# Keeping permuted token rows and gathering them as quarter rows for VectorE block transposes, in a pooling and expert-choice MoE layer

## What is computed

```
h = concat([meta, x])                        # 2064 x 1024
u = rmsnorm(h, norm_mix)
h = h + pool_mixer(u) * pool_scale           # windows 2, 4, 8, 16, then a 256x256 weight per group
u = rmsnorm(h, norm_ffn)
aff = softmax(u @ router_w)                  # 2064 x 16
for each expert e:
    g, idx = top_k(aff[:, e], 258)
    xs = u[idx]                              # 258 x 1024: the gathered rows
    hid = silu(xs @ w_gate[e]) * (xs @ w_up[e])      # 258 x 2048
    h[idx] += (hid @ w_down[e]) * g
return rmsnorm(h, norm_final)[16:]
```

## Time and profile before

| | |
|---|---|
| time, median of three runs | 2460.56 us |
| the profiled execution: its time | 2459.51 us |
| the profiled execution: its span | 2457.7 us |
| PE busy | 2386.0 us, 97% |
| PE weight loads busy | 2228.7 us, 91% |
| DVE busy | 1866.3 us, 76% |
| ACT busy | 1204.2 us, 49% |
| POOL busy | 850.4 us, 35% |
| DMA | 486.11 MB, mean 198 GB/s |

### The profile page before, as it was taken

The page is one execution under the profiler, slowest core; times in us unless marked ns, Lnnn a source line. Parts: engine busy times, 40 slices in busy tenths (PEclk is TensorE's granted clock), DMA queues, the critical chain, the costliest instruction groups (busy, mean ns, idle before and its releaser), DMA issues.

```text
span 2457.7 us, 48606 instructions
## 1 busy us (share of the span) xinstructions
PE 2386.0 (97%) x17338; PEld 2228.7 (91%) x17338; DVE 1866.3 (76%) x2259; ACT 1204.2 (49%) x1938; POOL 850.4 (35%) x1013
## 2 busy tenths in 40 slices
PE   7958999999999999999999999999999999999997
PEld 7947989898999989899998989899998989899997
DVE  5666786868787786968788686968778686968775
ACT  5653444444444444454444444454544444454464
POOL 0001525234251524335251524335152533425111
PEclk9968999999999999999999999999999999999998
DMA  7664648485765758586774848586674848576594
GB/s 239 213 194 128 185 135 257 151 244 183 212 198 154 227 148 251 159 237 173 204 214 140 246 139 248 160 239 188 181 216 136 253 142 251 171 227 199 159 346 164
DMA packets 345810, 486.11 MB, mean 198 GB/s; under 512 B 23117, under 2 KB 294997, under 8 KB 345778
## 3 DMA queue, kind: packets, MB, share of 16 engines
q1 hardware_dynamic: 318370, 433.82, 57.9%
q0 software_dynamic: 23232, 36.67, 6.9%
q10 hardware_dynamic: 4176, 15.21, 1.6%
HBM read 443.27 MB, written 46.31 MB: 199 GB/s over the span
## 4 chain that ended last, share of the span: by engine, by line
PE 87%; issue 3%; DVE 1%; POOL 1%; ACT 1%; DVEq 0%; POOLq 0%; ACTq 0%
PE bank L1498 86%; PE bank L1503 1%; ACT marks_a L910 0%; POOL fin L785 0%; POOL h_rows L793 0%; DVE w_lo L1340 0%; DVE h_rows L1459 0%; POOL fin L781 0%; POOL out L814 0%; DVE key_t L1223 0%; DVE x_lo L1345 0%; DVE y_rows L1450 0%; DVE marks_v L1197 0%; DVE flag L1204 0%; DVE cand L1210 0%
## 5 line engine op out<-in xcount | busy, mean ns | idle before, releaser
L1498 PE MATMUL bank<-x_hi,w_hi 128*128 128x258 f32 x4096 | 1156.8, 282 | 1.5 <-DVE x_lo L1345 1.5
L1498 PE MATMUL bank<-x_lo,w_hi 128*128 128x258 f32 x4096 | 1158.1, 283 | 0.0
L1498 PE MATMUL bank<-x_hi,w_lo 128*128 128x258 f32 x4096 | 1156.4, 282 | 0.0
L1340 DVE TENSOR_TENSOR w_lo<-raw,w_hi 128x1024 fp32r<-128x1024 f32 x584 | 713.9, 1223 | 116.5 <-ACT w_hi L932 91.0
L1498 PEld LDWEIGHTS bank<-x_hi,w_hi 128*128 128x128 f32 x4096 | 776.7, 190 | 15.0 <-issue 12.6
L1498 PEld LDWEIGHTS bank<-x_hi,w_lo 128*128 128x128 f32 x4096 | 778.1, 190 | 0.0
L1498 PEld LDWEIGHTS bank<-x_lo,w_hi 128*128 128x128 f32 x4096 | 777.4, 190 | 0.6
L932 ACT ACTIVATE w_hi<-raw 128x1024 fp32r<-128x1024 f32 x581 | 612.1, 1054 | 311.5 <-PE bank L1498 290.9
L668 POOL TENSOR_TENSOR carrier<-carrier 128x1 f32<-128x1 f32 x360 | 112.6, 313 | 1130.3 <-ACT y_rows L983 446.4
L713 POOL DMA_INDIRECT list_rows<-pair_now,slot_now x285 | 410.7, 1441 | 136.5 <-issue 135.6
L1366 DVE SCALAR_TENSOR_TENSOR acc_left<-raw,hid_left,acc_left 128x1024 f32<-128x1024 f32 x330 | 422.1, 1279 | 0.0
(11 more groups left out here) (209 smaller groups left out, 1893.1 us busy)
## 6 DMA issues: line engine op xcount, KB each, us to landing
raw<-in_moe_w_down SPq DMA_DIRECT2D x98, 1024.0 KB
raw<-in_moe_w_gate SPq DMA_DIRECT2D x97, 1024.0 KB
raw<-in_moe_w_up SPq DMA_DIRECT2D x97, 1024.0 KB
raw_more<-in_moe_w_gate SPq DMA_DIRECT2D x31, 1024.0 KB
raw_more<-in_moe_w_up SPq DMA_DIRECT2D x31, 1024.0 KB
raw_more<-in_moe_w_down SPq DMA_DIRECT2D x30, 1024.0 KB
h_in<-in_x SPq DMA_DIRECT2D x18, 512.0 KB, 5.7
h_acc<-h_mid SPq DMA_DIRECT2D x17, 448.0 KB, 4.9
```

The costliest lines, as they stand in the source:

```text
L1340: nc.vector.tensor_tensor(w_lo[:, a % 4], split_view(a, last), w_hi[:, a % 4].bitcast(f32), ALU.subtract).then_inc(split_lo, 1)
L1498: return nc.tensor.matmul(dst, lhs, rhs, start=start, stop=stop)
```

## The change

Rows of u are stored with their channels permuted. In the norm (DVE, stage one) four instructions of 256 columns write what one of 1024 wrote, and the router's weights are loaded in the same order by 16 DMAs. A row is seen as 4 quarters of 256 numbers. Nine indirect DMAs gather 128 quarter rows each (partition 32 i + c takes quarter i of token c of a group of 32) into `x_lanes`, which has the place of `x_rows`. DVE turns 32x32 blocks with three transposes of 128x768 (`turn_lanes`), after rows 10, 11 and 12 of `down`; ACT rounds (`round_lanes`, rows 11 to 13) and DVE subtracts (`rest_of_lanes`, rows 12 to 14) from SBUF. PE turns nothing of the gathered rows. The indices are quarter indices, `idx_lanes`: for the first expert 20 short instructions make them, later the list is read back with 10 DMAs instead of 3. `read_list` stands after row 1's `split_rest` and no longer ahead of row 0's work.

```diff
+GROUPS = 9
+PIECE = 3
...
-    u_chunks = u_rows.rearrange("t (m c) -> (t m) c", c=P)
+    u_quarters = u_rows.rearrange("t (i w) -> (t i) w", i=4)
...
-        x_rows = sb("x_rows", [P, 2, D], f32)
+        x_lanes = sb("x_rows", [P, GROUPS * 256], f32)
+        x_rows = x_lanes[:, 0:2 * D].rearrange("p (b d) -> p b d", b=2)
...
+        x_t = sb("x_t", [P, 2, PIECE * 256], f32, all_but_last)
...
+        def by_chunk(rows):
+            return rows.rearrange("p (i k r) -> p k i r", i=4, k=KD)
+        def in_order(rows):
+            return rows.rearrange("p (k i r) -> p k i r", i=4, k=KD)
...
-            sp.dma_start(rw[:], router_w[0].rearrange("(k p) e -> p k e", p=P)).then_inc(loaded_c, 16)
+            with nc.allow_non_contiguous_dma(reason="rows of 16 numbers"):
+                for j in range(4):
+                    for i in range(4):
+                        sp.dma_start(rw[32 * j:32 * j + 32, 2 * i:2 * i + 2, :],
+                                     router_w[0].rearrange("(h j i r) e -> j i r h e", h=2, j=4, i=4)[j, i])\
+                          .then_inc(loaded_c, 16)
...
-            def gather(first=False):
-                for b in range(2):
-                    pool.indirect_dma_start(x_rows[:, b, :], None, u_rows,
-                                            bass.IndirectOffsetOnAxis(ap=idx[:, b:b + 1], axis=0))\
-                        .then_inc(gathered[b], 16)
-                if first:
-                    pool.wait_ge(list_ready, 3)
-                pool.indirect_dma_start(x_left[0:SMALL_ROWS, :], None, u_chunks,
-                                        bass.IndirectOffsetOnAxis(ap=idx_chunk[0:SMALL_ROWS, :], axis=0))\
-                    .then_inc(gathered[2], 16)
+            def gather_lanes(first=False):
+                for g in range(GROUPS):
+                    if first and g % 8 == 0:
+                        pool.wait_ge(lanes_listed, 17 + g // 2)
+                    pool.indirect_dma_start(x_lanes[:, g * 256:(g + 1) * 256], None, u_quarters,
+                                            bass.IndirectOffsetOnAxis(ap=idx_lanes[:, g:g + 1], axis=0))\
+                        .then_inc(lanes_gathered[g // PIECE], 16)
...
-                    for t in range(LEFT):
-                        pool.dma_start(listed_rows[t:SMALL_ROWS:LEFT, 2, :],
-                                       list_rows[256 + t].partition_broadcast(KD)).then_inc(list_read, 16)
+                    pool.dma_start(listed_rows[0:LEFT, 2, :], list_rows[256:CAP, :]).then_inc(list_read, 16)
+                    for i in range(4):
+                        at = 32 * i
+                        pool.dma_start(listed_lanes[at:at + 32, 0:8, :],
+                                       list_rows[0:256, :].rearrange("(g c) v -> c g v", c=32)).then_inc(list_read, 16)
+                        pool.dma_start(listed_lanes[at:at + LEFT, 8, :], list_rows[256:CAP, :]).then_inc(list_read, 16)
...
-                pool.wait_ge(x_turned, XT * n + XT)
+                pool.wait_ge(lanes_turned, XP * n + XP)
                 carry_wait()
-                gather()
+                gather_lanes()
...
-            def round_x(i, done, at=0):
-                act.wait_ge(x_turned, done)
-                nc.scalar.activation(x_part(x_hi, i), turned_x(i, at), ACT.Copy).then_inc(x_hi_done, 1)
-            for i in range(XT):
-                round_x(i, i + 1, 4)
+            def round_lanes(m, p):
+                at = slice(96 * p, 96 * p + 96)
+                act.wait_ge(lanes_turned, XP * m + p + 1)
+                nc.scalar.activation(x_hi_wide[:, :, at].rearrange("p k (g c) -> p k g c", g=PIECE),
+                                     x_t[:, p % 2].rearrange("p (g k c) -> p k g c", g=PIECE, k=KD),
+                                     ACT.Copy).then_inc(x_hi_done, 1)
+            for p in range(XP):
+                round_lanes(0, p)
...
-                    if 8 <= k < 8 + XT:
-                        round_x(k - 8, XT * n + XT + k - 7)
+                    if 11 <= k < 11 + XP:
+                        round_lanes(n + 1, k - 11)
...
-                    nc.vector.scalar_tensor_tensor(out=u_out[:, s % 2, :], in0=h_mid[:, s % 2, :],
-                                                   scalar=inv2[:, s:s + 1], in1=nffn[:], op0=ALU.mult,
-                                                   op1=ALU.mult).then_inc(normed, 1)
+                    for i in range(4):
+                        ins = nc.vector.scalar_tensor_tensor(out=by_chunk(u_out[:, s % 2, :])[:, :, i],
+                                                             in0=in_order(h_mid[:, s % 2, :])[:, :, i],
+                                                             scalar=inv2[:, s:s + 1], in1=in_order(nffn[:])[:, :, i],
+                                                             op0=ALU.mult, op1=ALU.mult)
+                    ins.then_inc(normed, 1)
...
+                dve.wait_ge(list_ready, 1)
+                dve.wait_ge(lanes_listed, 1)
+                for i in range(4):
+                    for g in range(4):
+                        nc.vector.tensor_scalar(idx_lanes[32 * i:32 * i + 32, g:g + 5:4], idx[32 * g:32 * g + 32, 0:2],
+                                                4.0, float(i), ALU.mult, ALU.add).then_inc(lanes_listed, 1)
...
+                nc.vector.scalar_tensor_tensor(out=idx_lanes[:], in0=listed_lanes[:, :, 0], scalar=4.0,
+                                               in1=lane.broadcast_to([P, GROUPS]), op0=ALU.mult,
+                                               op1=ALU.add).then_inc(list_ready, 1)
...
-            def rest_of_x(i, count_, at=0):
-                dve.wait_ge(x_hi_done, count_)
-                nc.vector.tensor_tensor(x_part(x_lo, i), turned_x(i, at), x_part(x_hi, i).bitcast(f32),
+            def turn_lanes(m, p):
+                dve.wait_ge(lanes_gathered[p], 16 * PIECE * m + 16 * PIECE)
+                if p >= 2:
+                    dve.wait_ge(x_lo_done, XP * m + p - 1)
+                elif not isinstance(m, int):
+                    dve.wait_ge(x_lo_done, XP * m)
+                nc.vector.transpose(x_t[:, p % 2], x_lanes[:, p * PIECE * 256:(p + 1) * PIECE * 256])\
+                  .then_inc(lanes_turned, 1)
+            def rest_of_lanes(m, p):
+                at = slice(96 * p, 96 * p + 96)
+                dve.wait_ge(x_hi_done, XP * m + p + 1)
+                nc.vector.tensor_tensor(x_lo_wide[:, :, at].rearrange("p k (g c) -> p k g c", g=PIECE),
+                                        x_t[:, p % 2].rearrange("p (g k c) -> p k g c", g=PIECE, k=KD),
+                                        x_hi_wide[:, :, at].rearrange("p k (g c) -> p k g c", g=PIECE).bitcast(f32),
                                         ALU.subtract).then_inc(x_lo_done, 1)
...
-            for i in range(XT):
-                rest_of_x(i, i + 1, 4)
+            turn_lanes(0, 0)
+            turn_lanes(0, 1)
+            rest_of_lanes(0, 0)
+            turn_lanes(0, 2)
+            for p in range(1, XP):
+                rest_of_lanes(0, p)
...
-                read_list(n + 1)
                 for k in range(KF):
                     if k > 0:
                         split_rest(n, 32 + k + 3)
+                    if k == 1:
+                        read_list(n + 1)
                     add_left(n, 32 + k)
-                    if 8 <= k < 8 + XT:
-                        rest_of_x(k - 8, XT * n + XT + k - 7)
+                    if 12 <= k < 12 + XP:
+                        rest_of_lanes(n + 1, k - 12)
+                    if 10 <= k < 10 + XP:
+                        turn_lanes(n + 1, k - 10)
...
-            def turn_pair(i, at=0):
-                for k in (2 * i, 2 * i + 1):
-                    for b in range(2):
-                        col = k % 2 * 256 + b * P
-                        last = turn_block(bank[:, at + i, col:col + P], x_rows[:, b, k * P:(k + 1) * P])
-                last.then_inc(x_turned, 1)
-            def turn_left(m, at=0):
-                pe.wait_ge(x_lo_done, XT * m + 1)
-                turn_block(bank[:, at, 0:P], x_left[:]).then_inc(x_turned, 1)
...
+            pe.wait_ge(x_lo_done, XP)
...
-                    if k == 7:
-                        for landed in gathered:
-                            pe.wait_ge(landed, 16 * n + 32)
-                        turn_pair(0)
-                        turn_pair(1)
-                    if 8 <= k < 10:
-                        turn_pair(k - 6)
-                    if k == 10:
-                        turn_left(n + 1)
-                pe.wait_ge(x_lo_done, XT * n + 2 * XT)
+                pe.wait_ge(x_lo_done, XP * n + 2 * XP)
```

More of the change, by code:

```diff
@@ L121, in constants @@
     put("tok_hi", tok // 16)
-    put("chunk", k // LEFT)
+    put("lane", k // 32)
     quad = np.arange(2 * LEFT)
@@ L186, in encoder_kernel @@
         listed_rows = sb("listed_rows", [P, 3, 2], i32)
+        listed_lanes = sb("listed_lanes", [P, GROUPS, 2], i32)
+        idx_lanes = sb("idx_lanes", [P, GROUPS], i32)
```

(47 more changed lines are left out.)

24 lines of the change are left out of this document (7 added, 17 removed).

## The result

The changed kernel takes 2491.25 us (median of 4 runs, 2489.11 to 2493.45), the kernel before 2459.90 in the same comparison (4 runs, 2459.01 to 2460.71). The ratio is 1.0127, 95% interval 1.0115 to 1.0139: 31 us slower. Foretold were 2471, within 2450 to 2488. The profiled execution of the changed kernel took 2489.84 us, with a span of 2487.9, 30.2 more than before.

A forecast was written before the change was run, and what follows sets the result against it. PE was taken to bound the kernel, with 87% of the chain and busy throughout the expert loop. Terms -1 + 9.1 + 1 + 1 = +10.1 on the profiled 2459.5 gave 2469.6, or 2471 as a median; range 2450 to 2488.

The forecast's parts named there:

- the one that went over `gate_up` and the clock: In `gate_up`, late DVE does no harm and the pause ahead costs no clock: no time added.
- The pause itself: Ahead of `gate_up`, PE waits 1.8 us for x_lo, nearly cancelling 1.87 saved: -0.07 an expert, -1 us in all.
- R: The start of row 0 of `down` on PE, from which the forecast counts its times in the loop.
- rival 2: In the loop, a dear DVE transpose of 2.0 us makes the wait 5.2 and the kernel 2521; chance 0.10.
- The first gather: Before the first expert, index instructions, nine gathers and DVE's work start PE 9.1 us later, once; bounds +6 and +15.
- Stage one: Router weights' 16 DMAs delay the start, +1 (0 to 6); the norm's split writes add +1 (0 to 7.4).
- The list and the gather in the loop: POOL's ten list reads and nine later gathers in `down` land in time: no stall, cost nothing.
- rival 3: At DVE's `read_list`, the list lands late and holds up DVE, then PE; 4.2 us too late gives 2534; chance 0.06.
- Rival 1: Ahead of `gate_up`, the last x_lo is nearly in time: at 0.54 a transpose, wait 0.8, kernel 2455; chance 0.22.

The follow-up runs named there:

- a_early: Changed kernel with transposes, roundings and subtractions two rows of `down` earlier (transposes after rows 8 to 10): 2452.60 us, ratio 0.9974 to the kernel before.
- b_stride: Kernel before with only the rows of x_hi and x_lo set 288 numbers apart instead of 272: 2472.30 us against 2459.63, ratio 1.0056.

## Why the prediction was wrong

**The step that failed** is the one that went over `gate_up` and the clock. The text says "That a pause of this length costs the clock I don't assume" and leans on one pause of 1.20 us near the end of stage one. It foresaw 15 pauses of 1.8 us, half as long again as its one example, and took for them the value of that example, with no bound and no rival. The runs show that the clock falls after 4 of 15 such pauses, 1.5 us each time in block 0: 6 us. And it gave the products of `gate_up`, 87% of the chain with their like, no term at all, though the diff makes the rows of x_hi and x_lo, which each of them reads, 288 numbers apart instead of 272. That was the larger miss: 12.7 us by the run that changes nothing else. The two are 19 of the 20 us between the forecast 2471 and the measured 2491; either alone would have left the time inside the stated range. No row of the trace of before could have priced the distance; but an unpriced change of the operands of the bounding engine's products belonged in the range.

**The pause itself was right.** 1.8 a time was foretold, 1.9 came. The last x_lo ended at R + 46.12 where 45.97 was worked out, and PE started at 46.36 instead of 46.1. So `down` grew by 0.17 instead of shrinking by 0.07, which is +2.6 in 15 periods instead of -1. The transpose was priced at 0.87 and takes 0.90. The sum by the rate of the instructions that move one column in 1.04 ns held, and rival 2 at 2.0 did not come. The Trainium skill's VectorE: DVE Perf Modes (The three transpose paths) gives 311 ns for one 128x128 block of bf16. This form, float32 and six such blocks in one instruction, takes 0.90 for 128x768, 0.15 for each 128x128.

**The first gather was right in its total by luck, not in its parts.** +9.1 was foretold, and 10.06 - 0.96 = 9.1 came (0.96 is what the products of the list were late, 189.93 to 190.89). The 16 index instructions took 3.03, 0.19 each, where +1.2 (0.07 each) with a bound of 2.7 stood. In the loop short instructions do come 0.07 apart (idx_now, gates_now and idx_small at 455.67, 455.74 and 455.81); why these don't is open. POOL's first issue was at 200.44 instead of 197.3. What made up for it: the issues came 1.25 to 1.50 apart, against 1.44; from the ninth's issue to its landing (DVE's wait ends at 214.69) went 3.5 instead of 5, and 2.9 from there to PE instead of 2.8.

**Stage one** had +2 in two terms, and this pair of executions shows +0.96. The executions differ by more than that: the products of the list begin at 188.57 to 189.93 in the seven profiled kernels with the old stage one and at 189.73 to 192.51 in the nine with the new one, 2.0 later in the mean, as foretold. rw's 16 DMAs held SP's queue for 8.1 us:

```profile
7.53 8.08 SPq L547 DMA_DIRECT2D rw<-in_router_w  x16
15.65 0.43 SPq L530 DMA_DIRECT2D cst<-in_consts  x1
```

which is 0.5 a DMA against the 0.45 taken.

**The list and the gather in the loop** cost nothing, as foretold. POOL's ten reads and DVE's use of them:

```profile
445.50 0.77 POOL L726 DMA_DIRECT2D listed_rows<-list_rows  x1
...
450.76 0.54 POOL L733 DMA_DIRECT2D listed_lanes<-list_rows  x1
```

```profile
458.20 0.16 DVE L1349 SCALAR_TENSOR_TENSOR idx_lanes<-listed_lanes,lane_quad 128x9 int32<-128x9 int32 x1
```

DVE has no idle time ahead of it: rival 3 did not come. Rival 1, a last x_lo in time, did not come in this kernel because its rows were too late, not because of the price of a transpose; a_early shows that two rows earlier are enough. The prediction asked only how fast a transpose is, and took the rows of the schedule as given.

**The end** is shorter than before by 3.1 us (from the start of the last `down` to the end of the span 63.64 instead of 66.74). It was not foreseen, and by luck it brought the measured time nearer to the forecast. 2.0 of it lie behind the issue of the last DMA of the output: 9.9 us in all seven profiled kernels with the old code, 8.0 in all nine with the new. Why is not shown.

Together, by the traces of the two profiled executions: +2.6 in `down`, +13.4 for the distance in 16 experts (12.7 by the medians of b_stride), +6.2 for the clock, +1.1 in block 0 behind the pauses, +9.1 gather, +1.0 stage one, -3.1 at the end: 30.3, which is the difference of the spans.

## What to carry to other kernels

When work is moved off the bounding engine to another that then hands over late, look first at whether it can start earlier, and price the pause with the clock behind it, not the pause alone: here 31 us of pauses, from start to start, took 6 more with them, and two rows of the schedule turned 31 us lost into 7 us won. A change of the row distance of an operand that the bounding products read is a term of its own, even where no instruction is added; test it in the old kernel with one edited line. And where a change brings several costs at once, undo them one by one, and read each in its own stretch of the trace: a gain of 1.6 us at the start was plain there and lost in the times.

## What the runs showed of the hardware

- The rate of these products depends on the distance between the rows of x_hi and x_lo in the on-chip memory: 24 quarters of 24 products (576 products of 258 columns) take 69.06 us at 272 numbers and 69.71 at 288, 0.9%, with 69.09 at 264, 69.17 at 258, 69.30 at 280, 69.38 at 296 and 69.54 at 304. Moving the tensors as far with the distance kept leaves 69.06.
- The granted clock of PE fell from 1.00 to 0.50 behind 4 of 15 pauses of 1.9 us and 5 of 15 in another run of the same loop, none of 15 of 1.7, and all 15 of 4.5 or 4.7, each time 1.2 to 2.8 us of block 0. In the block shown it fell 1.3 us after the products had begun again; behind the pauses of 4.7 it was low from the first product on.
- Sixteen DVE instructions of 32x2 numbers, most of which read 32 partitions and write another 32, came 0.19 us apart; short copies over 128 partitions in the loop came 0.07 apart.
- DVE turns 32x32 blocks of 128x768 float32 in 0.90 us, near the rate of its subtraction of the same size (0.86 to 0.88 from start to start).
